# Second block's mixer: seven batches of transposes taken out of the attention loop and put in front of it

## The chip, the cores and the metric

The program runs on one core of one Trainium2 chip. The metric is device time of one execution in microseconds (us). PE is TensorE, ACT is ScalarE, DVE is VectorE, SP is the engine that issues the loads; PEld is the weight load of a PE instruction.

## The reference, cut to what matters

Two transformer blocks of two layers each, over 256 tokens and a width of 1024, in fp32. The change touches only the mixer of the second block, once in each of its two layers:

```
proj = n @ w_in                      # 2336 columns: latents, diff q/k/v, moba q/k/v
qh  = rmsnorm(c_q,  q_norm)  @ w_uq  # MLA queries (64 plain + 32 rotary columns, 6 heads)
kvh = rmsnorm(c_kv, kv_norm) @ w_ukv # MLA keys and values
o_b = diff_causal_attention(...)     # 6 heads, two softmaxes each: 6 units below
o_c = moba_causal_attention(...)     # 4 heads: 2 units
o_a = mla_causal_attention(...)      # 6 heads, queries and keys of 64 + 32: 4 units
return concat(o_a, o_b, o_c) @ w_out
```

Each attention is `softmax(q k^T * scale + bias) v` with a causal mask. For the score product PE wants queries and keys with the head's columns on the partitions, so these are first transposed ("turned") into a buffer QT.

## The kernel before, in words

Tokens lie on the partitions in two tiles (t = 0 and 1, 128 tokens each). A linear layer is a row of products `PS <- Wh,HTh`, `Wl,HTh`, `Wh,HTl` (lines 795 to 797): each weight piece is split by ACT (Wh, line 1314) and DVE (Wl, line 1702) into a high and a low part.

The mixer's attentions are 12 units run by one pipeline: units 0 to 5 are diff, 6 and 7 moba, 8 to 11 mla. An even unit is tile 0 (128 keys, one key block), an odd one tile 1 (256 keys, two key blocks). A unit has four heads, units 10 and 11 two. The steps of unit i:

- `scores(i)` on PE (line 931), into PSUM bank pair i % 2. It waits until mask(i - 2) has read that pair.
- `mask(i)` on DVE (lines 1868 or 1873, 1877, 1878): bias, row maximum, into SM. It waits for probs(i - 2), which read SM.
- `exps(i)` on ACT (line 1385): four exponentials with row sums.
- `probs(i)` on PE (line 943): four transposes for each key block, into PSUM bank 4 or 5 in turn. A counter x numbers everything that goes through these two banks; number x waits until number x - 2 has been copied out.
- `copies(i)` on ACT (line 1397): one copy for each key block, to PT.
- `values(i)` on PE (line 962): PT times the values, into bank 6 + i % 2.
- `end(i)` on DVE (lines 1886 to 1898): scale and store the output.

Each engine takes its own instructions strictly in the order in which they are written. PE's loop is scores(i), probs(i - 1), values(i - 2), for i from 1; units 0 and 1 have their scores ahead of it, in the middle of the last input projection. ACT's loop is exps(i), copies(i - 1). DVE's loop is mask(i), end(i - 2). At i = 0 ACT also takes the last projection out of PSUM (line 1358); at i = 4 ACT and DVE split one further weight piece (line 1314 between exps(4) and copies(3), line 1702 between mask(4) and end(2)).

The diff queries and keys are turned before the loop. The seven other batches (two for moba, five for mla; called turns below, or extras in the code) are inside it: turn k stands behind probs(k) on PE (line 951, four transposes of 128x128) and behind copies(k) on ACT (line 1404, one copy of 128x512 into QT, which lies in the buffer scr). They use the same banks 4 and 5 and the same counter x. Units 6 and 7 wait for turn 1, units 8 to 11 for turn 6.

Behind the loop PE turns the mixed rows (line 865) and goes on with the output projection. SP has a load of `mem` that waits for the last unit's values, and the next weights stand behind it in SP's queue.

Of the kernel before, what the change touches and what calls it, by code (L numbers as in the profile page):

```python
# [97 lines left out]
def build(nc, a, out):  # L98
    ctx = ExitStack()
    with ctx:  # L100
# [227 lines left out]
        def places(un):  # L328

            return list(range(4))[un["slots"]]  # L330

        def pt_order(units, extras, x):

            first, extra = [], []
            for i, un in enumerate(units):
                first.append(x)
                x += len(un["kbs"])
                for _ in extras.get(i, ()):
                    extra.append(x)
                    x += 1  # L340
            return first, extra, x

        def tok(t):
# [114 lines left out]
        def chunks_batch(chunks, slot, rows=P):  # L458

            return ([c for chunk in chunks for c in chunk], QT[0:rows, slot:slot + len(chunks), :], None)  # L460

        def plain_chunk(src, c0, n=P):

            return [src[:, t, c0:c0 + n] for t in range(T)]

        t_diff = []
        for c0, slot in ((DQ0, 0), (DK0, 4)):
            t_diff.append(chunks_batch([plain_chunk(proj, c0), plain_chunk(proj, c0 + P)], slot))
            t_diff.append(chunks_batch([plain_chunk(proj, c0 + 256, 64), plain_chunk(proj, c0 + 320, 64)], slot + 2, 64))
        t_moba = [chunks_batch([plain_chunk(proj, c0 + P * b) for b in range(2)], slot)  # L470
                  for c0, slot in ((MQ0, 8), (MK0, 10))]
# [2 lines left out]
        kr = [plain_chunk(H, 768)]  # L474
        mla_chunks = qn + qr + kn + kr
        t_mla = [chunks_batch(mla_chunks[k:k + 2], 12 + k) for k in range(0, 10, 2)]
        mix_extras = {i: [b] for i, b in enumerate(t_moba + t_mla)}

        def t_latent(layer):
            return [([proj[:, t, k * P:k * P + P] for t in range(T)], CQT[:, k:k + 1, :],  # L480
# [294 lines left out]
        def _(pe):  # L775
# [131 lines left out]
                c.misc += n  # L907
                pe.wait_ge(rows_ready, c.misc)

            def attention(units, extras={}):  # L910

                turns = c.turn
                u0, n = c.unit, len(units)
                first, extra, c.pt = pt_order(units, extras, c.pt)
                c.unit += n

                def scores(i):
                    u, un = u0 + i, units[i]
                    if i < 2:
                        pe.wait_ge(turn_out, turns)  # L920
                    if un["needs"]:
                        pe.wait_ge(pt_out, extra[un["needs"] - 1] + 1)
                    if u >= 2:
                        pe.wait_ge(sm_ready, u - 1)
                    at = places(un)
                    half = len(at) // 2
                    for pair in zip(range(half), range(half, 2 * half)) if at[half] == 2 else [(m,) for m in range(len(at))]:
                        for k in range(len(un["scores"][0])):
                            for m in pair:
                                q, key = un["scores"][m][k]  # L930
                                mm = pe.matmul(PS[:, 2 * (u % 2) + at[m] // 2, (at[m] % 2) * S:(at[m] % 2) * S + un["kl"]],  # L931
                                               q, key, start=(k == 0), stop=(k == len(un["scores"][m]) - 1))
                    mm.then_inc(sc_full, 1)

                def probs(i):
                    u, un = u0 + i, units[i]
                    pe.wait_ge(p_ready, u + 1)
                    for kb, size in enumerate(un["kbs"]):
                        x = first[i] + kb
                        if x >= 2:  # L940
                            pe.wait_ge(pt_out, x - 1)
                        for m in range(len(un["scores"])):
                            mm = pe.transpose(PS[0:size, 4 + x % 2, m * P:m * P + P],  # L943
                                              SM[:, u % 2, m, kb * P:kb * P + size], ident[:])
                        mm.then_inc(pt_full, 1)
                    before_x = sum(len(extras.get(k, ())) for k in range(i))
                    for x, (srcs, dst, _) in zip(extra[before_x:], extras.get(i, ())):
                        pe.wait_ge(pt_out, x - 1)
                        for k, s in enumerate(srcs):
                            rows, width = s.shape[0], s.shape[1]  # L950
                            mm = pe.transpose(PS[0:width, 4 + x % 2, k * P:k * P + rows], s, ident[0:rows, 0:rows])
                        mm.then_inc(pt_full, 1)

                def values(i):
                    u, un = u0 + i, units[i]
                    pe.wait_ge(pt_out, first[i] + len(un["kbs"]))
                    if u >= 2:
                        pe.wait_ge(o_out, u - 1)
                    dv = un["dv"]
                    for m, vs in enumerate(un["values"]):  # L960
                        for kb, v in enumerate(vs):
                            mm = pe.matmul(PS[:, 6 + u % 2, m * dv:(m + 1) * dv],  # L962
                                           PT[0:un["kbs"][kb], u % 2, kb, m, :], v,
                                           start=(kb == 0), stop=(kb == len(vs) - 1))
                    mm.then_inc(o_full, 1)

                def begin():
                    for i in range(2):
                        scores(i)

                def finish():
                    pe.wait_ge(lin_out, c.lin)
                    for i in range(1, n + 2):
                        if 2 <= i < n:
                            scores(i)
                        if i <= n:
                            probs(i - 1)
                        if i >= 2:
                            values(i - 2)
                    pe.wait_ge(o_out, u0 + n)  # L980

                return begin, finish
# [193 lines left out]
            for layer in range(LAYERS):  # L1176
# [44 lines left out]
                for step in attention(nsa_units()):  # L1221
                    step()
# [30 lines left out]
            for layer in range(LAYERS):  # L1253
# [35 lines left out]
                for step in attention(cross_units()):  # L1289
                    step()  # L1290
# [9 lines left out]
        def _(act):  # L1300
# [68 lines left out]
                        act.activation(dst, src, ACT.Copy, scale=gain).then_inc(turn_out, 1)  # L1369
                    c.turn += 1  # L1370

            def attention(units, extras={}, meanwhile={}):

                u0, n = c.unit, len(units)
                first, extra, c.pt = pt_order(units, extras, c.pt)
                c.unit += n

                def exps(i):
                    u, un = u0 + i, units[i]
                    act.wait_ge(sm_ready, u + 1)  # L1380
                    if u >= 4:
                        act.wait_ge(o_out, u - 3)
                    for m in range(len(un["scores"])):
                        row = SM[:, u % 2, m, 0:un["kl"]]
                        ins = act.activation(row, row, ACT.Exp, bias=nb[:, u % 2, m:m + 1], scale=un["scale"],  # L1385
                                             accum_out=sums[:, u % 4, m:m + 1])
                    ins.then_inc(p_ready, 1)

                def copies(i):
                    u, un = u0 + i, units[i]  # L1390
                    k = len(un["scores"])
                    for kb, size in enumerate(un["kbs"]):
                        x = first[i] + kb
                        act.wait_ge(pt_full, x + 1)
                        if u >= 2:
                            act.wait_ge(o_full, u - 1)
                        act.activation(PT[0:size, u % 2, kb, 0:k, :],
                                       PS[0:size, 4 + x % 2, 0:k * P].rearrange("p (m s) -> p m s", m=k),
                                       ACT.Copy).then_inc(pt_out, 1)
                    before_x = sum(len(extras.get(k, ())) for k in range(i))  # L1400
                    for x, (srcs, dst, _) in zip(extra[before_x:], extras.get(i, ())):
                        act.wait_ge(pt_full, x + 1)
                        cols_ = sum(s.shape[0] for s in srcs)
                        act.activation(dst, PS[0:dst.shape[0], 4 + x % 2, 0:cols_].rearrange(
                            "p (m s) -> p m s", m=dst.shape[1]), ACT.Copy).then_inc(pt_out, 1)

                for i in range(n + 1):
                    if i < n:
                        exps(i)
                    if i in meanwhile:  # L1410
                        meanwhile[i]()
                    if i >= 1:
                        copies(i - 1)

# [264 lines left out]
        def _(dve):  # L1679
# [167 lines left out]
                    dve.scalar_tensor_tensor(out=Y[:, ch, :], in0=src, scalar=w, in1=Y[:, ch, :],  # L1847
                                             op0=ALU.mult, op1=ALU.add).then_inc(conv_step, 1)

            def attention(units, extras={}, between=None):  # L1850

                u0, count = c.unit, len(units)
                first, _, c.pt = pt_order(units, extras, c.pt)
                c.unit += count

# [336 lines left out]
            for layer in range(LAYERS):  # L2192
# [89 lines left out]
                    convolve((taps - early) * (i + 1) // n - (taps - early) * i // n)  # L2282

                c.turn += 2 + 2 + 1 + 6 + 1
                attention(nsa_units(), {}, between)

                c.lin = base + 14
                bank = bank_of()
# [172 lines left out]
```

## Time and profile before

| | us |
|---|---|
| median of 3 runs | 2657.15 (2653.49 to 2657.33) |
| the profiled execution, its own time | 2661.76 |
| its span in the trace | 2660.0 |
| mixer's loop, first layer: first probs to scores(8) | 1765.50 to 1812.64 |
| mixer's loop, second layer: the same | 2239.32 to 2287.96 |

Times in the trace count from the span's start. In a timeline row the first number is the start, the second the time from that start to the end of the group, and a bracket gives the idle time of the engine just before it and what ended it. A product of fp32 operands shows as two instructions in the trace, so a unit's four heads are x8 in scores (mla: x16) and x8 for each key block in values; a transpose shows as one. The clock column is TensorE's granted clock as a share of 2.4 GHz: 1.00 is 2.4 GHz, 0.50 is 1.2 GHz.

### The profile page before, as it was taken

The page shows a single profiled execution, that of the slowest core. Times are in us where ns is not written, and L with a number is a line of the kernel's source. Part 1 is how long each engine was busy: PE and PEld are TensorE (multiplying, and loading weights), DVE is VectorE, ACT ScalarE, POOL GpSimd, SP SyncE. Part 2 cuts the span into 40 slices and gives each one's busy share as a digit, 9 for nine tenths or more (in the row PEclk, how much of TensorE's full clock was granted, in tenths as well). Part 3 has the DMA queues.
Part 4 walks back from the last instruction along what each step waited for, and adds up shares of the span by engine and source line. Part 5 has one row for each costly group of instructions (what it writes and reads, how often), then busy time and mean ns, then how long its engine had stood idle before and what let it go on. Part 6 is the DMA issues. An engine that isn't in the chain of part 4 may idle for free.

```text
span 2660.0 us, 31787 instructions
## 1 busy us (share of the span) xinstructions
PE 2544.0 (96%) x11894; PEld 2132.8 (80%) x11894; DVE 1812.6 (68%) x2378; ACT 1475.1 (55%) x1807; POOL 48.6 (2%) x70
## 2 busy tenths in 40 slices
PE   7899999989899999999999999989989999898998
PEld 5788888878788888888888888777878887787887
DVE  5756444675688888889898888744545564454654
ACT  5334443633577777777777777553544445344443
POOL 0000000000000000000000000000000000000000
PEclk8859999976799999999999999986999998599999
DMA  7304555320399999999999999612535542163551
GB/s 223 125 1 143 190 190 190 97 96 32 134 372 349 368 341 377 342 371 347 352 367 347 367 349 369 211 48 105 186 106 190 190 147 76 47 222 111 179 185 55
DMA packets 250692, 565.24 MB, mean 212 GB/s; under 512 B 8992, under 2 KB 23776, under 8 KB 250592
## 3 DMA queue, kind: packets, MB, share of 16 engines
q1 hardware_dynamic: 250592, 563.90, 60.1%
q8 instruction: 63, 1.03, 0.2%
q14 instruction: 37, 0.30, 0.0%
HBM read 562.82 MB, written 1.05 MB: 212 GB/s over the span
## 4 chain that ended last, share of the span: by engine, by line
PE 84%; issue 7%; DVE 5%; ACT 2%; POOL 1%; DMA 0%; DVEq 0%; POOLq 0%; ACTq 0%
PE PS L795 23%; PE PS L797 22%; PE PS L796 22%; PE PS L931 4%; PE PS L962 4%; PE PS L943 2%; PE PS L1089 1%; PE PS L1123 1%; PE PS L865 1%; PE PS L1097 1%; DVE scr L1847 1%; PE PS L874 1%; ACT SM L1385 1%; PE PS L1016 0%; PE PS L854 0%
## 5 line engine op out<-in xcount | busy, mean ns | idle before, releaser
L2075 DVE TENSOR_TENSOR Wl<-ring,Wh 128x2048 fp32r<-128x2048 f32 x334 | 760.1, 2291 | 105.8 <-ACT Wh L1493 105.7
L1493 ACT ACTIVATE Wh<-ring 128x2048 fp32r<-128x2048 f32 x334 | 639.5, 1917 | 131.5 <-PE PS L797 131.5
L1702 DVE TENSOR_TENSOR Wl<-ring,Wh 128x2048 fp32r<-128x2048 f32 (+3 forms) x194 | 435.8, 2252 | 332.9 <-ACT Wh L1314 332.6
L1314 ACT ACTIVATE Wh<-ring 128x2048 fp32r<-128x2048 f32 (+3 forms) x194 | 365.3, 1891 | 271.5 <-PE PS L797 271.5
L795 PE MATMUL PS<-Wh,HTh 128*128 128x512 f32 (+3 forms) x1184 | 467.4, 395 | 23.7 <-DVE Wl L1702 14.0
L797 PE MATMUL PS<-Wh,HTl 128*128 128x512 f32 (+3 forms) x1184 | 461.3, 390 | 0.0
L796 PE MATMUL PS<-Wl,HTh 128*128 128x512 f32 (+3 forms) x1184 | 461.2, 390 | 0.0
L795 PE MATMUL PS<-Wh,xgh 128*128 128x512 f32 x896 | 354.6, 396 | 2.5 <-DVE xgl L1709 2.5
L797 PE MATMUL PS<-Wh,xgl 128*128 128x512 f32 x896 | 350.4, 391 | 0.0
L796 PE MATMUL PS<-Wl,xgh 128*128 128x512 f32 x896 | 349.8, 390 | 0.0
L795 PEld LDWEIGHTS PS<-Wh,HTh 128*128 128x128 f32 x1184 | 226.5, 191 | 69.1 <-issue 11.0
L797 PEld LDWEIGHTS PS<-Wh,HTl 128*128 128x128 f32 x1184 | 225.9, 191 | 44.2
L796 PEld LDWEIGHTS PS<-Wl,HTh 128*128 128x128 f32 x1184 | 226.3, 191 | 42.5
L795 PEld LDWEIGHTS PS<-Wh,xgh 128*128 128x128 f32 x896 | 168.8, 188 | 36.1 <-issue 2.7
L797 PEld LDWEIGHTS PS<-Wh,xgl 128*128 128x128 f32 x896 | 168.5, 188 | 35.8
L796 PEld LDWEIGHTS PS<-Wl,xgh 128*128 128x128 f32 x896 | 168.9, 189 | 33.8
L1385 ACT ACTIVATE SM<-SM,nb 128x256 f32<-128x256 f32 (+2 forms) x200 | 84.6, 424 | 179.9 <-DVE nb L1878 179.9
L795 PE MATMUL PS<-Wh,hmh 128*128 128x512 f32 x448 | 175.2, 391 | 0.0
L797 PE MATMUL PS<-Wh,hml 128*128 128x512 f32 x448 | 174.6, 390 | 0.0
L796 PE MATMUL PS<-Wl,hmh 128*128 128x512 f32 x448 | 174.6, 390 | 0.0
L795 PE MATMUL PS<-Wh,hTh 128*128 128x512 f32 x368 | 143.8, 391 | 0.0
L797 PE MATMUL PS<-Wh,hTl 128*128 128x512 f32 x368 | 143.4, 390 | 0.0
(283 smaller groups left out, 2919.1 us busy)
## 6 DMA issues: line engine op xcount, KB each, us to landing
ring<-in_moe_w_gate SPq DMA_DIRECT2D x112, 1024.0 KB, 7.1
ring<-in_moe_w_up SPq DMA_DIRECT2D x112, 1024.0 KB, 7.2
ring<-in_moe_w_down SPq DMA_DIRECT2D x112, 1024.0 KB, 6.7
ring<-in_mlp_w SPq DMA_DIRECT2D x64, 1024.0 KB, 5.1
ring<-in_w_in SPq DMA_DIRECT2D x28, 1024.0 KB, 6.1
ring<-in_w_out SPq DMA_DIRECT2D x16, 1024.0 KB, 5.2
ring<-in_cross_wkv SPq DMA_DIRECT2D x16, 1024.0 KB, 10.5
ring<-in_ffn_w_gate SPq DMA_DIRECT2D x14, 1024.0 KB, 5.1
```

The lines of the kernel that those rows point to most:

```text
L795: pe.matmul(out_, hi, high, start=start, stop=False)
L796: pe.matmul(out_, hi, low, start=False, stop=False)
L797: return pe.matmul(out_, lo, high, start=False, stop=stop)
L865: mm = pe.transpose(PS[0:width, c.turn % 4, off:off + rows], s, ident[0:rows, 0:rows])
L931: mm = pe.matmul(PS[:, 2 * (u % 2) + at[m] // 2, (at[m] % 2) * S:(at[m] % 2) * S + un["kl"]], q, key, start=(k == 0), stop=(k == len(un["s ...
L943: mm = pe.transpose(PS[0:size, 4 + x % 2, m * P:m * P + P], SM[:, u % 2, m, kb * P:kb * P + size], ident[:])
L962: mm = pe.matmul(PS[:, 6 + u % 2, m * dv:(m + 1) * dv], PT[0:un["kbs"][kb], u % 2, kb, m, :], v, start=(kb == 0), stop=(kb == len(vs) - 1))
L1314: act.activation(Wh[:, i % SPLITS, 0:n], ring[:, r % RING, 0:n], ACT.Copy).then_inc(w_hi, 1)
L1385: ins = act.activation(row, row, ACT.Exp, bias=nb[:, u % 2, m:m + 1], scale=un["scale"], accum_out=sums[:, u % 4, m:m + 1])
L1493: act.activation(Wh[:, (base + i) % SPLITS, :], ring[:, (raw + i) % RING, :], ACT.Copy).then_inc(e_hi, 1)
L1702: dve.tensor_tensor(Wl[:, i % SPLITS, 0:n], ring[:, r % RING, 0:n], Wh[:, i % SPLITS, 0:n].bitcast(F32), ALU.subtract).then_inc(w_lo, 1)
L2075: dve.tensor_tensor(Wl[:, (base + i) % SPLITS, :], ring[:, (raw + i) % RING, :], Wh[:, (base + i) % SPLITS, :].bitcast(F32), ALU.subtract) ...
```

## The change

All seven turns run ahead of the loop: on PE behind the wait for the last projection's banks and before probs(0), on ACT behind the last projection's copies and before exps(1). Their numbers x come first (0 to 6), and probs of unit 0 begins at x = 7. Nothing else moves; there are as many instructions as before. The first block's attention and the cross attention pass no extras and keep their order.

```diff
         def pt_order(units, extras, x):
 
-            first, extra = [], []
-            for i, un in enumerate(units):
+            extra = list(range(x, x + len(extras)))
+            x += len(extras)
+            first = []
+            for un in units:
                 first.append(x)
                 x += len(un["kbs"])
-                for _ in extras.get(i, ()):
-                    extra.append(x)
-                    x += 1
             return first, extra, x
...
-        mix_extras = {i: [b] for i, b in enumerate(t_moba + t_mla)}
+        mix_extras = t_moba + t_mla
...
-                    before_x = sum(len(extras.get(k, ())) for k in range(i))
-                    for x, (srcs, dst, _) in zip(extra[before_x:], extras.get(i, ())):
+
+                def turns_ahead():
+
+                    for x, (srcs, dst, _) in zip(extra, extras):
                         pe.wait_ge(pt_out, x - 1)
...
                 def finish():
                     pe.wait_ge(lin_out, c.lin)
+                    turns_ahead()
                     for i in range(1, n + 2):
...
-                    before_x = sum(len(extras.get(k, ())) for k in range(i))
-                    for x, (srcs, dst, _) in zip(extra[before_x:], extras.get(i, ())):
+
+                def turns_ahead():
+
+                    for x, (srcs, dst, _) in zip(extra, extras):
                         act.wait_ge(pt_full, x + 1)
...
                     if i in meanwhile:
                         meanwhile[i]()
+                    if i == 0:
+                        turns_ahead()
                     if i >= 1:
                         copies(i - 1)
```

PE at the head of the loop, before: probs are `PS<-ident,SM`, turns `PS<-ident,proj` (also scr and H), scores `PS<-scr`, values `PS<-proj,PT`.

```order
L797 MATMUL PS<-Wh,HTl 128x384
L943 MATMUL PS<-ident,SM 128x128 x4
L951 MATMUL PS<-ident,proj 128x128 x4
L931 MATMUL PS<-scr 128x128 x4
L943 MATMUL PS<-ident,SM 128x128 x8
L951 MATMUL PS<-ident,proj 128x128 x4
L962 MATMUL PS<-proj,PT 128x64 x4
L931 MATMUL PS<-scr 128x256 x4
L943 MATMUL PS<-ident,SM 128x128 x4
L951 MATMUL PS<-ident,proj 128x128 x4
L962 MATMUL PS<-proj,PT 128x64 x8
```

The same place in the changed kernel:

```order
L952 MATMUL PS<-ident,proj 128x128 x14
L952 MATMUL PS<-ident,scr 128x128 x6
L952 MATMUL PS<-ident,H 128x128 x8
L942 MATMUL PS<-ident,SM 128x128 x4
L930 MATMUL PS<-scr 128x128 x4
L942 MATMUL PS<-ident,SM 128x128 x8
L963 MATMUL PS<-proj,PT 128x64 x4
L930 MATMUL PS<-scr 128x256 x4
L942 MATMUL PS<-ident,SM 128x128 x4
L963 MATMUL PS<-proj,PT 128x64 x8
```

The 28 transposes of the seven turns stand together, and values(i - 2) follows probs(i - 1) directly.

ACT at the head of its loop, before: exponentials write `SM,sums`, copies of probabilities `PT<-PS`, copies of turns `scr<-PS`.

```order
L1385 ACTIVATE SM,sums<-SM,nb 128x128 x4
L1358 ACTIVATE proj<-PS,row_rs 128x384 x2
L1385 ACTIVATE SM,sums<-SM,nb 128x256 x4
L1397 ACTIVATE PT<-PS 128x512
L1404 ACTIVATE scr<-PS 128x512
L1385 ACTIVATE SM,sums<-SM,nb 128x128 x4
L1397 ACTIVATE PT<-PS 128x512 x2
L1404 ACTIVATE scr<-PS 128x512
```

The same place in the changed kernel:

```order
L1387 ACTIVATE SM,sums<-SM,nb 128x128 x4
L1360 ACTIVATE proj<-PS,row_rs 128x384 x2
L1408 ACTIVATE scr<-PS 128x512 x7
L1387 ACTIVATE SM,sums<-SM,nb 128x256 x4
L1399 ACTIVATE PT<-PS 128x512
L1387 ACTIVATE SM,sums<-SM,nb 128x128 x4
L1399 ACTIVATE PT<-PS 128x512 x2
```

The seven copies stand between the projection's and exps(1). DVE's instructions keep their order.

## Rows read from the trace of the kernel before

**Rows 1.** The page, part 1: busy time and share of PE.

```profile
PE 2544.0 (96%) x11894; PEld 2132.8 (80%) x11894; DVE 1812.6 (68%) x2378; ACT 1475.1 (55%) x1807; POOL 48.6 (2%) x70
```

**Rows 2.** Windows: both mixer loops up to scores(8), then the first block's attention.

```profile
1764.50:1812.60 48.10, 35.98 (x190) 30.83 (x188) 22.24 (x61) 24.01 (x75) 0.00 (x0) 0.64 0.00 1
2238.30:2288.00 49.70, 37.77 (x192) 32.33 (x190) 22.24 (x61) 24.02 (x75) 0.00 (x0) 0.57 0.00 1
602.00:610.00 8.00, 8.00 (x31) 6.68 (x29) 4.65 (x20) 2.61 (x10) 0.00 (x0) 0.50 0.00 0
```

**Rows 3.** Timeline of PE in the first layer's loop.

```profile
1765.50 0.63 PE L943 MATMUL PS<-ident,SM 128*128 128x128 f32 x4 [0.72 <-issue]
1765.97 0.60 PE L951 MATMUL PS<-ident,proj 128*128 128x128 f32 x4
...
1767.99 1.06 PE L943 MATMUL PS<-ident,SM 128*128 128x128 f32 x8 [0.78 <-ACT PT L1397]
1771.28 1.12 PE L951 MATMUL PS<-ident,proj 128*128 128x128 f32 x4 [2.22 <-ACT PT L1397]
...
1773.92 2.08 PE L931 MATMUL PS<-scr 32*128 32x256 f32 x8
...
1777.69 3.52 PE L962 MATMUL PS<-proj,PT 128*128 128x64 f32 x16
1781.14 1.23 PE L931 MATMUL PS<-scr 32*128 32x128 f32 x8
1782.29 1.97 PE L943 MATMUL PS<-ident,SM 128*128 128x128 f32 x8
1788.22 0.69 PE L951 MATMUL PS<-ident,proj 128*128 128x128 f32 x2 [3.96 <-ACT PT L1397]
...
1812.64 2.98 PE L931 MATMUL PS<-scr 64*128 64x128 f32 x16 [2.32 <-ACT scr L1404]
```

**Rows 4.** Timeline of ACT in the same loop.

```profile
1767.27 0.58 ACT L1397 ACTIVATE PT<-PS 128x512 f32<-128x512 f32 x1
...
1784.24 0.40 ACT L1385 ACTIVATE SM<-SM,nb 128x128 f32<-128x128 f32 x1 [2.25 <-DVE nb L1878]
...
1785.80 1.89 ACT L1314 ACTIVATE Wh<-ring 128x2048 fp32r<-128x2048 f32 x1
...
1795.90 0.51 ACT L1385 ACTIVATE SM<-SM,nb 128x256 f32<-128x256 f32 x1 [5.93 <-DVE nb L1878]
...
1797.88 0.57 ACT L1397 ACTIVATE PT<-PS 128x512 f32<-128x512 f32 x1
1798.36 0.57 ACT L1404 ACTIVATE scr<-PS 128x512 f32<-128x512 f32 x1
```

**Rows 5.** Timeline of DVE in the same loop.

```profile
1782.41 0.88 DVE L1873 SCALAR_TENSOR_TENSOR SM<-dist,PS 128x128 f32<-128x128 f32 x4
...
1787.72 2.29 DVE L1702 TENSOR_TENSOR Wl<-ring,Wh 128x2048 fp32r<-128x2048 f32 x1 [3.51 <-ACT Wh L1314]
1790.98 0.18 DVE L1886 RECIPROCAL coef<-sums 128x4 f32<-128x4 f32 x1 [0.96 <-PE PS L962]
...
1791.84 0.29 DVE L1898 TENSOR_TENSOR H<-otmp 128x128 f32<-128x128 f32 x1
1792.99 1.41 DVE L1873 SCALAR_TENSOR_TENSOR SM<-dist,PS 128x256 f32<-128x256 f32 x4 [0.86 <-PE PS L931]
```

**Rows 6.** Timeline of PE in the second layer's loop.

```profile
2239.32 0.63 PE L943 MATMUL PS<-ident,SM 128*128 128x128 f32 x4 [0.72 <-issue]
...
2287.96 2.98 PE L931 MATMUL PS<-scr 64*128 64x128 f32 x16 [2.75 <-ACT scr L1404]
```

**Rows 7.** Timeline of SP's queue at the end of the first layer's loop.

```profile
1842.61 0.37 SPq L698 DMA_DIRECT2D scr<-in_mem  x1
```

**Rows 8.** Windows: the clock in the second layer's loop, and behind it.

```profile
2242.20:2243.20 1.00, 1.00 (x7) 0.94 (x5) 0.64 (x2) 0.29 (x1) 0.00 (x0) 0.50 0.00 0
2324.00:2328.00 4.00, 4.00 (x12) 3.09 (x12) 3.93 (x11) 0.59 (x1) 1.56 (x1) 0.58 1.06 394
```

More of the change, by code:

```diff
@@ L908, in rows, with attention @@
                 pe.wait_ge(rows_ready, c.misc)
-            def attention(units, extras={}):
+            def attention(units, extras=()):
                 turns = c.turn
@@ L1370, in turn, with attention @@
                     c.turn += 1
-            def attention(units, extras={}, meanwhile={}):
+            def attention(units, extras=(), meanwhile={}):
                 u0, n = c.unit, len(units)
@@ L1848, in conv_ops, with attention @@
                                              op0=ALU.mult, op1=ALU.add).then_inc(conv_step, 1)
-            def attention(units, extras={}, between=None):
+            def attention(units, extras=(), between=None):
                 u0, count = c.unit, len(units)
@@ L2284, in _ @@
                 c.turn += 2 + 2 + 1 + 6 + 1
-                attention(nsa_units(), {}, between)
+                attention(nsa_units(), (), between)
                 c.lin = base + 14
```

## The prediction

> **What bounds the kernel now.** I read the page's busy shares first, then the windows of the two places that the change touches, then the timelines of PE, ACT and DVE in them. PE is busy 96% of the span [rows 1], so only PE's own work and its gaps count. In the mixer loops it is different: PE is busy 36.0 of 48.1 us in the first layer and 37.8 of 49.7 in the second, with a granted clock of 0.64 and 0.57 [rows 2], that is 1.2 GHz for most of the stretch. ACT and DVE are below half. So the loop is bound by PE at the low clock plus waits of PE.
>
> The timeline shows where the waits are [rows 3]. Behind probs(1), and again behind probs(3), the turn waits 2.22 and 3.96 us for ACT: the turn's bank must first be copied out, and that copy stands behind the exponentials of the next unit. Behind the waiting turn stand values(i-2) and scores(i+1), which had nothing to wait for, and then DVE and ACT wait in their turn for these scores (5.93 us ahead of the exponentials at 1795.90 [rows 4]). One more wait, 2.32 us and 2.75 us, stands ahead of scores(8), which needs the last turn's copy [rows 3, 6].
>
> **The change part by part.** I write all times from the first instruction behind the last projection (0 is 1765.50 in the first layer, 2239.32 in the second). Before, scores(8) starts at 47.1 and 48.6 [rows 3, 6]. From there on the order is unchanged, so the shift of scores(8) is the gain of a layer.
>
> Durations at the low clock: probs or a turn of four 0.9 (half of 1.97 less its tail of 0.2, at 1782.29), of eight 1.75; scores of 128 keys 1.15, of 256 keys 2.0; values of x16 3.45, of x8 half that, 1.75 [rows 3]. mask of 128 keys 1.85 (1782.41 to the exponentials at 1784.24), of 256 keys 2.9 (1792.99 to 1795.90); exps of 128 keys 1.55 (1784.24 to 1785.80), of 256 keys 2.0 (1795.90 to 1797.88); a copy 0.48 behind another one and 0.58 to its end; ACT's weight split 1.8, DVE's 2.3; end 1.15 (1790.98 to the end of the instruction at 1791.84) [rows 4, 5].
>
> *The seven turns in front.* At the high clock a turn takes 0.60 to its end [rows 3], its copy 0.58 [rows 4], and the bank comes back 0.14 after the copy ends (1767.85 to 1767.99). With two banks that is 1.34 for two turns. probs(0) needs the sixth turn's copy: 0.5 for the second bank's offset, three rounds of 1.34 = 4.5, call it 4.6. exps(1), behind the seventh copy, starts at 5.3. Nothing hides this: PE and ACT would have been in the loop. This is the price.
>
> *The loop behind it.* probs(0) 4.6, scores(2) 5.1. exps(1) 5.3 to 7.3. probs(1) 7.45 to 9.2, values(0) to 10.9, scores(3) to 13.0. mask(3) 13.2, exps(3) 16.2 to 18.1. PE meanwhile does probs(2), values(1), scores(4) and reaches 18.5, so probs(3) starts there with no gap; values(2) to 22.0, scores(5) to 24.0. ACT: exps(4) 20.6 to 22.2, its split to 24.0; DVE: split to 26.4, end(2) to 27.6, then mask(5) to 30.5, exps(5) 30.6 to 32.6. PE has scores(6) behind it by 30.1 and waits 2.6 for exps(5): a new, late wait, on DVE's split instead of on the turn. probs(5) 32.7, values(4) 34.5, scores(7) 36.2, probs(6) 38.2, values(5) 39.1, scores(8) 42.6.
>
> Against before, the landmarks are: scores(3) 10.9 against 8.4 (2.5 late), scores(4) 17.3 against 15.6 (1.7 late), then ahead, and scores(8) 42.6 against 47.1: **4.5 us gained in the first layer**. In the second layer the clock had fallen by 2242.20, 2.9 us in [rows 8]; there the last two turns run at 1.12 to their end instead of 0.60, which puts scores(8) at 43.2 against 48.6: **5.4 us gained**. Together 9.9, call it 10.
>
> The same can be seen from what goes away: seven turns of PE work inside the loop (6.3 at the low clock) and the waits of 2.2, 4.0, about 2.2 (behind probs(5), the third place) and 2.3, in all some 17; less 5 in front, the new wait of 2.6, about 2 because parts that ran at the high clock now run at the low one, and 2 of ACT's and DVE's latency that the old waits covered.
>
> *Behind the loop.* The load of `mem`, with the next weights behind it, is issued when the last values are done [rows 7]; it moves earlier by the same amount, as PE does. I cost it at nothing. The clock there is uncertain: in the second layer the next projection still runs at 0.58 in its first 4 us [rows 8]. A low clock in such a stretch costs up to 1.9, so each layer may win or lose that. I take 0.
>
> *A page against the row.* In the trace the last PE work before the loop is at the high clock, and the clock falls some 3 to 6 us behind it, with turns and probs already running; the turns seen before that ran at 0.60 [rows 3]. The Trainium skill (TensorE: Matmul & The Clock Gate, Part 4: PE-mode transpose) says that transposes do not count as PE work for the clock gate. Read so, 28 transposes in a row are idleness, and the clock falls inside them; the rows can't decide, since no stretch of before has that many. That result is rival A.
>
> The profiled execution took 2661.76, its span 2660.0; it lies 4.6 above the median. I apply the difference to the median: 2657.15 - 10 = **2647**.
>
> **The rivals.**
>
> A, the low clock from the first turn. Each round of two then takes 1.12 + 0.58 + 0.14 = 1.84 [rows 3, 4], so probs(0) is at 6.2 instead of 4.6; scores(8) comes at 44.2 and the gain is 2.9 + 4.4 = 7.3: 2650. For it: the second layer's clock fell after 2.9. Against: the first layer held it for longer than the seven turns need.
>
> B, the clock comes back in the loop, since its gaps are gone. Against: the first block's attention has no gaps at all and runs at 0.50 throughout [rows 2]. For: the loop had two short stretches at the high clock before, and they may stay. If one such stretch of about 3.5 us stays in each layer the gain is 13.5 (2643.5); if the whole loop ran at the high clock, the same ledger at half durations puts scores(8) at 34, a gain of some 27 (2630).
>
> C, slower. The loop is not bound by PE but by the ring scores, mask, exps, probs: 2.0 + 0.2 + 2.9 + 2.0 is 7.1 for an odd unit, and PE would have had to wait there anyway. PE's own work between scores(i) and probs(i) is 0.9 + 3.45 + 1.15 = 5.5, mask and exps with hand-overs 5.3, so only 0.2 separates the two. If ACT or DVE take longer than that margin at every unit, the old waits return at probs, the front costs 4.6 to 6.2, and only scores(8)'s wait of 2.3 to 2.75 is saved: +2 to +4 a layer, 2661 to 2665. It decides where mask and exps exceed 5.5. Against: the first block's attention, PE busy 8.00 of 8.00 [rows 2].
>
> D, the gain is taken back by the split at unit 4. ACT's copies(3) and DVE's mask(5) both stand behind it. If the turns' lateness of 1.7 is still there when the split begins and the DVE wait grows from 2.6 to 5, the gain is 2 to 2.5 a layer: 2652.5. Against: in the ledger exps(4) is reached before PE needs it.
>
> **How the numbers follow.** Forecast 0.62, A 0.13, B 0.12 (0.03 of it whole), C 0.05, D 0.08. The forecast's own range is 8 to 13 us gained, 2644 to 2649.5, with the clock behind the loop as its spread. The medians of three scatter by some 2 either way. The range that leaves 2 in 10 out reaches from B's short stretches to D: 2640 to 2653. What this measurement can tell from no change is 0.2%, 5.3 us: faster is forecast, A nearly whole, B: 0.84. D, and what is left of A: 0.11. C: 0.05.
>
> **What would show it.** In the changed profile: seven turns in 4.5 to 5 us, probs(0) at 4.6; no wait ahead of values behind probs(1), (3), (5); none ahead of scores(8); one wait of 2 to 3 us ahead of probs(5), released by ACT, which waited for DVE; scores(8) at 42 to 44 in both layers; PE busy over nine tenths of the loop from probs(1) on. A first stretch over 6 us means A; a clock over 0.55 in the loop behind the turns means B; gaps ahead of probs(3) as well mean C. Wrong would be a scores(8) later than 46.

## The result and the profile after

| | us |
|---|---|
| before, median of 20 runs | 2657.5 (2652.0 to 2660.9) |
| changed, median of 20 runs | 2641.0 (2612.3 to 2649.1) |
| ratio changed / before | 0.9925 (0.9905 to 0.9944) |
| the profiled execution: own time, span | 2629.57, 2627.9 |

The kernel is faster. The forecast was a gain of 10 us; the medians differ by 16.5 and the ratio says 19.9 (0.0075 x 2657.5). The median lies at the lower end of the stated range of 2640 to 2653, and 2637.6, which the ratio gives, lies under it. The time also spreads over 37 us, where before spread over 9. With the six executions of the run *again* below there are 26. Sorted by time they form groups, of which the last two nearly touch, and the slower a group, the lower its mean granted clock: two at 2612 (0.945), five at 2629 to 2634 (0.934 to 0.936; these two are called the low groups below), nine at 2638 to 2642 (0.930 to 0.934), ten at 2643 to 2649 (0.927 to 0.932).

The profiled execution shows both kinds of loop, one in each layer. First layer, PE, in answer to [rows 3]; columns as there:

```profile
1761.20 1.06 PE L952 MATMUL PS<-ident,proj 128*128 128x128 f32 x8 [0.72 <-issue]
1762.51 0.93 PE L952 MATMUL PS<-ident,proj 128*128 128x128 f32 x6 [0.25 <-ACT scr L1408]
...
1765.20 0.66 PE L952 MATMUL PS<-ident,H 128*128 128x128 f32 x4 [0.20 <-ACT scr L1408]
1765.78 0.63 PE L942 MATMUL PS<-ident,SM 128*128 128x128 f32 x4
1766.34 0.71 PE L930 MATMUL PS<-scr 32*128 32x128 f32 x8
1768.50 1.14 PE L942 MATMUL PS<-ident,SM 128*128 128x128 f32 x8 [1.45 <-ACT SM L1387]
1769.47 1.44 PE L963 MATMUL PS<-proj,PT 128*128 128x64 f32 x8
1770.85 2.08 PE L930 MATMUL PS<-scr 32*128 32x256 f32 x8
...
1792.10 1.97 PE L942 MATMUL PS<-ident,SM 128*128 128x128 f32 x8 [2.16 <-ACT SM L1387]
...
1798.51 3.52 PE L963 MATMUL PS<-proj,PT 128*128 128x64 f32 x16
1801.96 2.98 PE L930 MATMUL PS<-scr 64*128 64x128 f32 x16
```

The turns take 4.58 us to probs(0), at the high clock throughout. The waits behind probs(1), (3), (5) and ahead of scores(8) are gone. What is left is 1.45 us ahead of probs(1), 0.45 ahead of probs(4) and 2.16 ahead of probs(5). scores(8) comes 40.8 us after the first turn; before it was 47.1.

Why the wait ahead of probs(5) is there, in ACT's and DVE's rows (answering [rows 4, 5]):

```profile
1781.87 1.89 ACT L1316 ACTIVATE Wh<-ring 128x2048 fp32r<-128x2048 f32 x1
...
1789.98 0.51 ACT L1387 ACTIVATE SM<-SM,nb 128x256 f32<-128x256 f32 x1 [5.25 <-DVE nb L1884]
```

```profile
1783.80 2.29 DVE L1708 TENSOR_TENSOR Wl<-ring,Wh 128x2048 fp32r<-128x2048 f32 x1 [3.51 <-ACT Wh L1316]
...
1787.08 1.41 DVE L1879 SCALAR_TENSOR_TENSOR SM<-dist,PS 128x256 f32<-128x256 f32 x4
```

It is the weight split in front of mask(5), as forecast. Second layer, PE, in answer to [rows 6]:

```profile
2263.92 2.08 PE L930 MATMUL PS<-scr 64*128 64x256 f32 x8
2265.93 1.11 PE L942 MATMUL PS<-ident,SM 128*128 128x128 f32 x4
2266.83 2.56 PE L963 MATMUL PS<-proj,PT 128*128 128x64 f32 x16
2269.32 1.75 PE L930 MATMUL PS<-scr 64*128 64x128 f32 x16
2271.08 1.13 PE L942 MATMUL PS<-ident,SM 128*128 128x128 f32 x8
...
2287.79 1.96 PE L864 MATMUL PS<-ident,H 128*128 128x128 f32 x16 [0.58 <-DVE H L1900]
```

The same 16 products of scores(8) take 1.75 instead of 2.98. In values(5), at 2266.83, the clock rises to 2.4 GHz, and it stays there to the loop's end. The windows from scores(8) on, first layer and second layer (columns: window, length, busy time of PE, PEld, DVE, ACT, POOL, clock, DMA share, GB/s):

```profile
1801.90:1832.40 30.50, 30.00 (x135) 24.15 (x134) 13.15 (x54) 10.42 (x37) 2.26 (x1) 0.50 0.00 1
2269.30:2287.70 18.40, 16.99 (x135) 13.32 (x134) 13.04 (x54) 11.12 (x41) 2.26 (x1) 1.00 0.01 1
```

The same 135 instructions in 30.5 us at 0.50 and in 18.4 us at 1.00. The whole way from the first instruction to the turns behind the loop is 71.3 and 58.6 us, against 77.7 and 79.2 before: 27.0 of the 32.1 us by which the two profiled spans differ. 4.3 lie ahead of the first loop, which the change does not touch.

So there are two effects: the loop is shorter without any return of the clock, as the first layer shows, and in some executions the clock comes back in it.

### The profile page after: what moved, and what is told of

It is laid out like the page before. It is cut to its first block, busy times and chain, and to the rows that moved or that the text cites. A ratio compares the mean times of both kernels' runs of the same rounds, so it can differ in the third digit from the quotient of the medians.

```text
span 2627.9 us, 31787 instructions
## 1 busy us (share of the span) xinstructions
PE 2524.7 (96%) x11894; PEld 2115.9 (81%) x11894; DVE 1811.8 (69%) x2378; ACT 1475.0 (56%) x1807; POOL 48.6 (2%) x70
## 4 chain that ended last, share of the span: by engine, by line
PE 84%; issue 8%; DVE 5%; ACT 2%; POOL 1%; DMA 0%; DVEq 0%; POOLq 0%; ACTq 0%
PE PS L794 23%; PE PS L796 23%; PE PS L795 23%; PE PS L930 4%; PE PS L963 4%; PE PS L942 2%; PE PS L1091 1%; PE PS L1125 1%; PE PS L1099 1%; DVE Wl L1708 1%; PE PS L864 1%; DVE scr L1853 1%; PE PS L873 1%; ACT SM L1387 1%; PE PS L1018 0%
```

## The experiments

The theories were: **gap** (a high clock that starts about values(5) is ended by PE's wait ahead of scores(8); without that wait it lasts to the loop's end), **density** (what counts is that the loop's other waits are gone) and the plain **sum** of the prediction, with no return of the clock.

**again**: the changed kernel once more, unchanged.

> The changed kernel once more, as the yardstick on this chip. Both theories: 2612 to 2649 us, in groups by whether the high clock comes back in no layer's loop (about 2647), in one (about 2630) or in both (about 2612); the median about 2641, ratio to before 0.990 to 0.995.

Measured 2643.6 (2629.0 to 2646.7), ratio 0.9939 (0.9921 to 0.9958). Its profiled execution has no return in either layer: scores(8) at 40.6 and 40.4, the loops 71.1 and 70.9 us long, its time 2643.2. This is the low-clock case by itself.

**e1_last_turn_back**: six turns in front, the seventh in its old place. `extras` becomes a table by place, with -1 for the front; the later kernels use it too.

```diff
-        mix_extras = t_moba + t_mla
+        mix_extras = {-1: (t_moba + t_mla)[:6], 6: t_mla[-1:]}
...
                         if i <= n:
                             probs(i - 1)
+                            turn_extras(i - 1)
```

> Six turns in front, the seventh behind the probabilities of unit 6 as before, so scores(8) waits for its copy again. Gap theory (a high clock that starts about values(5) is ended by PE's wait ahead of scores(8), and without that wait lasts to the loop's end): the wait of some 2 us is there, each layer about 1.5 us longer, and the clock is never high in the mla units: all executions 2646 to 2653. Density theory (what matters is that the waits behind probs(1), (3), (5) are gone): spread and median as the changed kernel, 2612 to 2650, about 2642. Sum theory (the seven turns' work only, no clock): 2647 to 2650.

Measured 2639.5 (2638.2 to 2641.2). No expectation is met whole: no execution lies in the low groups, as gap says, but the level is 7 us under gap's; it is density's level, without its spread. In its trace scores(8) comes at 38.6 in both layers, with a wait of 0.83 us ahead of it in the first and of 2.95 us in the second. The clock had fallen some 7 us later than in the changed kernel, in both layers. In the second it rose again 33 us after the start and was low 7 us later, within scores(8), behind the wait of 2.95. That trace fits gap, the times decide nothing.

**e2_no_wait_at_8**: the old places, but the last two turns both behind unit 5.

```diff
-        mix_extras = {i: [b] for i, b in enumerate(t_moba + t_mla)}
+        mix_extras = {i: [b] for i, b in enumerate((t_moba + t_mla)[:5])}
+        mix_extras[5] = t_mla[-2:]
```

> The old order, one turn behind probs of units 0 to 4, and two behind unit 5, none behind unit 6: the waits behind probs(1), (3), (5) stay, the one ahead of scores(8) is gone. Gap theory: the clock comes back about values(5) and stays in part of the executions: times from 2620 to 2655, some at least 10 us below the fastest of before. Density theory: clock low through the mla units as before, all 2650 to 2658 (the wait of 2.3 at most is saved in each layer).

Measured 2625.8 (2624.3 to 2627.4), ratio 0.9884 (0.9869 to 0.9898): 15 us under the changed kernel, with all the waits that the change had removed, except the one ahead of scores(8). Density is out. Gap had expected a spread; here all four executions are low.

**e3_pause_only**: the changed kernel with a wait more.

```diff
+                    if un["needs"] == 7 and i == 8:
+                        pe.wait_ge(p_ready, u)
```

> The changed kernel with one wait more and nothing moved: in both layers PE waits ahead of scores(8) until the exponentials of unit 7 are done, some 2 to 3 us. Gap theory: no high clock in the mla units, all executions 2647 to 2654. Density theory: as the changed kernel plus 4 to 6 us, with the same spread, 2617 to 2654.

Measured 2644.8 (2642.9 to 2645.0). None of five executions is in the low groups, as gap says, but all lie under the 2647 to 2654 that it expected, and inside the range of density. It is weak in any case: without any effect five executions would miss the low groups one time in five (19 of 26 miss them). At the low clock the wait is only 0.78 us long. In its trace the clock comes back in neither layer, and at the loop's head it falls 8.8 us after the start in the first layer and 16.5 in the second. Up to scores(8) the loop's instructions are those of the changed kernel, so the place of that fall varies too, with nothing changed in the loop ahead of it.

**e4_two_at_5_and_pause**: e2 with the same two lines.

> The kernel of e2_no_wait_at_8 (2624 to 2627 us) with one wait more and nothing moved: PE waits ahead of scores(8) until the exponentials of unit 7 are done. Gap theory: the high clock that starts about values(5) is ended by this wait and the mla units run at 1.2 GHz again: 10 to 12 us lost in each layer, 2646 to 2653. Order theory (e2 is fast because two turns stand behind unit 5, not for the missing wait): at most 2 to 3 us lost in each layer, 2626 to 2632.

Measured 2659.6 (2655.5 to 2662.9), ratio 1.0008 (1.0000 to 1.0017), 11 executions. **One wait in each layer costs 33.8 us**, more than gap expected. PE in the first layer of e2:

```profile
1806.27 1.95 PE L971 MATMUL PS<-proj,PT 128*128 128x64 f32 x16
1808.15 1.75 PE L938 MATMUL PS<-scr 64*128 64x128 f32 x16
1810.51 1.14 PE L950 MATMUL PS<-ident,SM 128*128 128x128 f32 x8 [0.61 <-ACT SM L1396]
```

and of e4:

```profile
1805.17 1.90 PE L973 MATMUL PS<-proj,PT 128*128 128x64 f32 x16
1809.47 2.98 PE L940 MATMUL PS<-scr 64*128 64x128 f32 x16 [2.40 <-issue]
1812.37 1.97 PE L952 MATMUL PS<-ident,SM 128*128 128x128 f32 x8
```

The profile finds no releaser for the wait of 2.40 ("issue"); it stands where the added line is.

values(5) runs at the high clock in both (1.95 and 1.90). With nothing behind it to wait for, the clock stays; after a wait of 2.40 us it is low, and stays low to the end. The windows from scores(8) on in this layer, of e2:

```profile
1808.20:1827.20 19.00, 16.91 (x135) 13.27 (x134) 13.13 (x55) 11.47 (x41) 2.26 (x1) 1.00 0.00 1
```

and of e4:

```profile
1809.50:1840.00 30.50, 29.92 (x135) 24.13 (x135) 12.13 (x50) 9.52 (x33) 2.26 (x1) 0.50 0.00 1
```

The second layer of e4 is another case, again from values(5) on:

```profile
2280.66 3.52 PE L973 MATMUL PS<-proj,PT 128*128 128x64 f32 x16
2284.97 2.98 PE L940 MATMUL PS<-scr 64*128 64x128 f32 x16 [0.79 <-issue]
```

Here the clock does not come back at all, values(5) takes 3.52, and the wait is 0.79. So that a wait ends the high clock is seen in the first layer only; in the second the rise is missing, though the loop's instructions up to there are those of e2, and why is open.

The loops are 63.8 and 64.0 us long in e2, 77.8 and 79.2 in e4, the latter as before. The two profiled spans differ by 35.0 us: 29.1 in the loops, 7.1 behind them, less 1.2 ahead of the first. The turns' places alone (e4 against before) are worth nothing; the 33.8 us come with the added wait, since nothing else differs.

**e5_turns_behind_scores**: e2's places, and each turn on PE moved behind the scores that used to stand behind it.

```diff
                         if 2 <= i < n:
                             scores(i)
+                            turn_extras(i - 2)
                         if i <= n:
                             probs(i - 1)
-                            turn_extras(i - 1)
```

> The old distribution over the units (two turns in unit 5, none in 6), but each turn issued behind the scores of the next unit but one instead of ahead of them, so that neither values nor scores stand behind a waiting turn: no waits in the loop but the one ahead of probs(5), no turns in front. Ledger at the low clock: as the changed kernel, +6.3 of turns in the loop, -4.6 in front: about 2645 to 2650. If the clock comes back at values(5) as in e2_no_wait_at_8 and holds: 2620 to 2626. Gap theory says that it holds if it comes; whether it comes is what this run asks.

Measured **2598.8** (2597.8 to 2601.1), ratio 0.9779 (0.9767 to 0.9792). It beats both kernels, 59 us under before and 42 under the changed one, and lies more than 20 under the better of its two expectations. scores(8) comes at 34.2 and 31.1, the loops are 52.6 and 49.4 us long. The windows of its first layer:

```profile
1763.50:1779.00 15.50, 11.97 (x101) 10.06 (x102) 8.78 (x27) 13.14 (x42) 0.00 (x0) 1.00 0.00 1
1779.00:1796.00 17.00, 15.83 (x75) 13.79 (x76) 11.80 (x31) 7.88 (x25) 0.00 (x0) 0.51 0.00 1
1797.70:1816.00 18.30, 16.86 (x135) 13.33 (x134) 13.06 (x54) 9.58 (x35) 2.26 (x1) 1.00 0.00 1
```

The turns are spread, so nothing delays probs(0); the waits are 1.6 us at most; and the clock is high in the first 15 us and again from values(5) on, where the expectation had only the second. In the second layer it is high for 11 us and again from 25 on.

**e6_split_at_9**: the changed kernel, the weight split moved to unit 9, on ACT and in DVE's `between` alike.

```diff
-                          {0: lambda: take_block(4), 4: another})
+                          {0: lambda: take_block(4), 9: another})
```

> The changed kernel with the weight split of ACT and DVE moved from unit 4 to unit 9. Takes away the wait of 2.2 us ahead of probs(5). PE theory: 2 us gained in each layer in every execution, median 2637 with the spread of the changed kernel. If waits in the diff and moba units are needed for the clock to come back, the low group of executions (2612 to 2630) is gone and all lie at 2639 to 2645.

Measured 2632.0 (2631.4 to 2633.8), ratio 0.9906 (0.9892 to 0.9921): 9 to 12 us under the changed kernel's medians, but the intervals overlap (0.9905 to 0.9944 there), so four executions do not settle the size. scores(8) comes at 37.9 and 35.5. Neither the low group nor the level of 2639 to 2645 came. In the trace the clock comes back in both layers, from 43 to 53 us in the first and from 32 to 39 in the second, and holds to the end in neither.

**e7_no_wait_at_8_split_at_9**: e2 with the same move of the split.

> The kernel of e2_no_wait_at_8 with the weight split moved from unit 4 to unit 9. The wait of 3.97 us behind probs(3) shrinks by the split's 1.8 on ACT and DVE's 2.3: 2 to 4 us gained in each layer if the clock comes back as it did, 2617 to 2623. If the place of the rise depends on the lengths ahead of it, the clock may come back later or not at all: up to 2648.

Measured 2648.3 (2635.8 to 2651.3): the second case of the expectation. Less waiting ahead, and 22 us slower than e2. scores(8) comes at 43.0 instead of 44.8 in the first layer, but the rest of the loop takes 30.0 instead of 19.1. The clock is high through scores(8), with no wait ahead of it, and falls behind a wait of 1.08 us ahead of probs(7):

```profile
1808.27 1.75 PE L938 MATMUL PS<-scr 64*128 64x128 f32 x16
1811.11 1.49 PE L950 MATMUL PS<-ident,SM 128*128 128x128 f32 x8 [1.08 <-ACT SM L1396]
1812.39 1.81 PE L971 MATMUL PS<-proj,PT 128*128 128x64 f32 x8
```

That is against the second half of gap: without the wait ahead of scores(8) the high clock need not last to the loop's end.

**e8_behind_scores_split_at_9**: e5 with that move.

> The kernel of e5_turns_behind_scores (2598 to 2601 us) with the weight split moved from unit 4 to unit 9. Ledger: the waits around unit 3 and 5 shrink, 0 to 3 us gained in each layer: 2593 to 2599. Against it stands e7, where the same move made the clock come back later: then 2600 to 2625.

Measured 2610.3 (2605.6 to 2614.3), 11.5 us slower than e5, though scores(8) of the first layer is early, at 26.4. It is not the case of e7: in the first layer the clock is high from the start to 39.5 us, in the second it falls and comes back where it does in e5, at 11 and 25. The high clock ends at a wait that e5 does not have, in the middle of probs(9), in the second layer within that wait and in the first 0.8 us behind it:

```profile
1803.72 0.66 PE L950 MATMUL PS<-ident,SM 128*128 128x128 f32 x4 [1.62 <-ACT PT L1408]
```

ACT's split, moved to unit 9, now stands ahead of the copy that frees the bank. So the move does not take a wait away, it puts one in another place, and in e6 the same wait of 1.62 stands ahead of the fall in the first layer. The loops are 51.1 and 56.1 us long, against 52.6 and 49.4: 5.2 of the 10.9 us by which the two profiled spans differ.

**e9_filled_waits**: the changed kernel with three products more in each layer, which nothing uses.

```diff
+                    for _ in range({1: 1, 5: 2}.get(i, 0) if un["kbs"][0] == P and len(units) == 12 and units[0]["end"][0] == "diff" else 0):
+                        pe.wait_ge(pt_out, first[i] - 1)
+                        pe.matmul(PS[:, 4 + first[i] % 2, :], ident[:], X[:, 0, 0:512], start=True, stop=True)
                     pe.wait_ge(p_ready, u + 1)
```

> The changed kernel with three dummy products of 128x128 by 128x512 fp32 (results overwritten, so nothing of the output changes), one in the wait ahead of probs(1) and two in the wait ahead of probs(5), 0.5 us each at the high clock and 1 us at the low one. If PE's waits are what lowers the clock: it falls later and comes back in more executions, median 2615 to 2635. If waits do not matter and only the work's own kind does: as the changed kernel, 2640 to 2648.

Measured 2618.5 (2603.9 to 2622.0), ratio 0.9845 (0.9819 to 0.9870): **added work makes the kernel 23 to 25 us faster** than the changed one (0.9905 to 0.9944). The two dummy products ahead of probs(5), and what stands behind them:

```profile
1791.38 3.51 PE L938 MATMUL PS<-X,ident 128*128 128x512 f32 x4
1794.73 1.04 PE L945 MATMUL PS<-ident,SM 128*128 128x128 f32 x8
1795.61 1.00 PE L966 MATMUL PS<-proj,PT 128*128 128x64 f32 x8
```

They take 3.5 us at the low clock, longer than the wait they fill, and from their end the high clock holds for 17 us, through scores(8), where PE does not wait. At the loop's head it fell some 7 us later than in the changed kernel, with the one dummy product ahead of the fall; but e1 and the second layer of e3 fell as late without one. Whether it is the filled wait or the kind of product, four times as wide as a transpose, that brings the clock back, this run can't tell apart. On its way the high clock outlives a wait as long as the one in e7, at the same place:

```profile
1802.76 1.14 PE L945 MATMUL PS<-ident,SM 128*128 128x128 f32 x8 [1.08 <-ACT SM L1390]
1803.73 1.00 PE L966 MATMUL PS<-proj,PT 128*128 128x64 f32 x8
```

and it ends behind one of 0.72 us ahead of probs(9), a wait that e2, e5 and the second layer of the changed kernel have there too and outlive. So the length of the last wait does not decide alone.

**e10_behind_scores_filled**: e5 with one such product ahead of probs(3) and one ahead of probs(5).

> The kernel of e5_turns_behind_scores with one such dummy product ahead of probs(3) and one ahead of probs(5), in waits of 1.6 and 1.2 us. If waits lower the clock: 2588 to 2597. If not: 2598 to 2603.

Measured 2603.5 (2595.4 to 2605.6), over e5's 2598.8; the ranges overlap, so no gain is to be had here that five executions show. In its trace the clock is high for the first 22 us, longer than in e5, but PE then waits 4.12 us ahead of the second dummy product.

**e11_behind_scores_pause**: e5 with the wait of e3 and e4.

> The kernel of e5_turns_behind_scores with PE waiting ahead of scores(8) until the exponentials of unit 7 are done, nothing moved. Gap theory: the high clock that starts about values(5) is ended there, 10 to 12 us lost in each layer: 2616 to 2626. Without a clock effect the wait costs 2 to 3 us in each layer: 2602 to 2607.

Measured 2605.6 (2601.1 to 2607.8): the case without a clock effect at this place. The two turns of unit 5 stand between scores(7) and the wait, which is therefore 0.22 us in the first layer and 1.40 in the second:

```profile
2242.09 1.90 PE L973 MATMUL PS<-proj,PT 128*128 128x64 f32 x16
2245.39 1.75 PE L940 MATMUL PS<-scr 64*128 64x128 f32 x16 [1.40 <-issue]
```

Behind it the products still run at the high clock (1.75). So of two waits at the same place the one of 2.40 us ended the high clock and the one of 1.40 did not. The second layer is 55.6 us long instead of 49.4 mostly for another reason: the clock at its head fell after 2.5 us, in e5 after 11.5.

## Why the prediction was wrong

Two terms of the sum failed, and both are TensorE's clock: how long it stays high at the loop's head, and that it never comes back behind it. The mean of the 26 executions is 2638.4, 19.2 us under before (mean 2657.6), where 10 were forecast. The 19 outside the low groups have a mean of 2643.1, a gain of 14.5; the seven others bring the rest. So each term makes about half of the miss, if the seven are the ones in which the clock came back and held.

*What bounds the loop*: right. PE at the low clock plus PE's waits, and the waits that it named were the ones that went.

*The seven turns in front*: right. probs(0) at 4.58, forecast 4.6; exps(1) at 5.2 (1766.39), forecast 5.3.

*The loop behind it*: right in mechanism, by two to three microseconds too slow. The one new wait, ahead of probs(5) behind DVE's split, was forecast at 2.6 and is 2.16. scores(8) was forecast at 42.6 and 43.2 and comes at 40.6 and 40.4 in an execution in which the clock does not come back. The mis-sized term is where the clock falls. The ledger had it low from probs(1) on at 7.45, in the second layer from 2.9 on, since before it had fallen by 5.8 and 2.9. It fell 8.3 to 9.1 us after the start in the four layers with a trace, within or just behind values(0) (1.44 in the rows above, between 1.00 and 1.81). In the first layer of *again* scores(3) so came at 9.5 where the ledger had 10.9, which is 1.4 of the 2.0 us there. In the low-clock case the loops are 71.1 and 70.9 instead of 77.7 and 79.2, a gain of 14.9 in the traces where 9.9 was forecast. The prediction's second count, by what goes away, comes to 17 - 11.6 = 5.4 for a layer, a little over the ledger's 4.5 of the first; it did not show the term either.

*A page against the row*, rival A (0.13): it did not come. In four layers with a trace all 28 transposes ran at the high clock, and it lasted longer than before. The Trainium skill (TensorE: Matmul & The Clock Gate, Part 4: PE-mode transpose) says that the full clock does not engage for transposes, which do not count as busy in the same way. The trace does not agree in so far as 28 of them in a row ran at the full clock, which wide products ahead of them had left; whether transposes can raise a low clock no run here shows.

*Rival B* (0.12): **this is the other step that failed.** The forecast's ledger ran at the low clock to the loop's end. The argument against B was the first block's attention, dense and at 0.50 [rows 2]. That row is true, and 30.0 of 30.5 us busy at 0.50 in the changed kernel say the same: a full PE alone did not bring the clock back in such work. But the question was another one. Before, the clock did come back for some 3.5 us about values(5), in both layers. These are two windows of the kernel before, at values(5) of the second layer and behind it, in the wait ahead of scores(8) [rows 6]:

```profile
2283.00:2284.00 1.00, 1.00 (x11) 1.00 (x10) 0.97 (x3) 0.00 (x0) 0.00 (x0) 1.00 0.00 0
...
2287.00:2288.00 1.00, 0.04 (x2) 0.04 (x2) 0.00 (x0) 0.91 (x2) 0.00 (x0) 0.50 0.00 0
```

In both the clock fell within that wait. e2 against e4 shows what the wait does: with it the time is 33.8 us longer, and in the first layer of e4 the high clock ends there. The prediction priced that wait at its length, 2.3. The change removes it. In the one layer with a trace in which the clock rose about values(5) it stayed and saved 12 us: 30.5 against 18.4 from scores(8) on. By the groups of times that happens in one layer in 5 of 26 executions and in both in two; that each group is what its mean clock suggests is inferred, since only two of the executions have a trace. In the changed kernel itself the test is e3, and it is weak.

*Behind the loop*, taken as 0: there it is small. Between the two loops the changed kernel's profiled execution is 0.6 us longer than that of before, behind the second 1.4 shorter.

*Rivals C and D*: neither came. Behind the turns PE waited over 1 us at two places, ahead of probs(1) and probs(5), and the split's wait is smaller than forecast.

What stays open is what starts the high clock in the middle of the loop, and what ends it in general. In e2 it rises at the same two places of both layers, 36 and 43 us after the start, in e4 in the first layer only, in the changed kernel only in some executions, and in e7 elsewhere. The first of the two rises of e2, and of the first layer before, begins in the wait behind probs(5) and ends while PE is busy, 1.7 us after that wait: so a fall need not stand in the wait itself. A wait of 1.08 us stands ahead of the fall in e7 and not in e9. That the clock depends on the work and the waits ahead of it is all that the runs show.

## What to carry to other kernels

Where TensorE runs at two clocks, a wait can cost far more than its length: look in the granted clock for short rises, see which wait stands at the end of each, and try first without that one. Here one wait in each layer, 2.40 us long where the trace shows it at work, was worth 34 us, and moving a turn with the wait kept was worth nothing (e4 against before). Then look where the next wait comes to stand, since e7 and e8 lost the high clock at a later one. Put turns behind the products that do not need them, not in front of the loop (e5, 2598.8 against 2641.0), and judge such an edit by many executions, since their spread, 37 us here, tells more than their median.

## What the runs showed that was not expected

- 28 transposes in a row ran at the high clock, 0.5 us for four, and it did not fall in them.
- Three products more in each layer made the kernel 23 to 25 us faster (e9).
- Moving one weight split from unit 4 to unit 9 cost 22 us in e7 and 11.5 in e8. In e6 the median is 9 to 12 us lower, with intervals that overlap. In e7 PE waited less ahead of scores(8); in e8 the split made a new wait of 1.62 us.
- The Trainium skill (TensorE: Matmul & The Clock Gate, Why this matters for your kernels) advises to keep TensorE continuously busy to reach the full clock. In the first layer's loop of the changed kernel PE was busy 30.00 of 30.50 us and the clock stayed at 1.2 GHz: there small products with their weight loads filled the time and did not raise it. In the second layer the same products held the full clock once it was there (1.00).
